# GpSimd subtracts the high parts of four weight chunks, and VectorE skips them

## What is computed

```
x = x + 0.5 * swiglu(rmsnorm(x, ff1_norm), ...)
h = rmsnorm(x, mix_norm);  proj = h @ w_in          # the mixer begins
...
y = gla_mixer(x, ...)                               # second block, layer 0
x = layer_norm(ALPHA * x + y, ...)
x = layer_norm(ALPHA * x + swiglu_ffn(x, ...), ...)
y = moba_mixer(x, positions, w_in, w_out)           # layer 1: block attention begins
...
```

## Time and profile before

| | |
|---|---|
| median of three runs | 1213.64 us (1212.88 to 1213.91) |
| the profiled execution's own time | 1213.54 us |
| its span, first to last instruction | 1211.5 us |
| TensorE busy | 1199.9 us (99%) |
| VectorE busy | 942.8 us (78%) |
| ScalarE busy | 678.2 us (56%) |
| GpSimd busy | 42.1 us (3%), 85 instructions |
| low parts of weights on VectorE (line 1765) | 476.6 us, 405 instructions, mean 1196 ns |

### The profile page before, as it was taken

How to read it: one execution, slowest core, us unless ns; L and a number is a source line. 1 busy time by engine, 2 the same in 40 slices (tenths; PEclk the granted TensorE clock), 3 DMA queues, 4 the chain that set the end, 5 groups by cost and what they waited for, 6 DMA issues and landing times.

```text
span 1211.5 us, 16276 instructions
## 1 busy us (share of the span) xinstructions
PE 1199.9 (99%) x6097; PEld 1008.9 (83%) x6097; DVE 942.8 (78%) x1396; ACT 678.2 (56%) x973; POOL 42.1 (3%) x85
## 2 busy tenths in 40 slices
PE   9999999999999999999999999999999999999997
PEld 7888888888788888888888888888887888888886
DVE  5999997756676666888987677786998777687797
ACT  6566655546666354665656554656554454566561
POOL 2000002100000000000010001000000000000000
PEclk9999999999999999999999999999999999999999
DMA  8666566754545556666557656566566544766652
GB/s 271 198 207 193 184 208 199 251 174 142 155 141 173 184 181 208 176 194 187 191 180 187 193 192 221 170 194 196 174 209 216 167 139 139 238 181 194 187 189 72
DMA packets 150654, 225.83 MB, mean 186 GB/s; under 512 B 8152, under 2 KB 85984, under 8 KB 150576
## 3 DMA queue, kind: packets, MB, share of 16 engines
q1 hardware_dynamic: 148048, 216.10, 56.8%
q0 software_dynamic: 2512, 8.69, 2.6%
q10 hardware_dynamic: 16, 0.00, 0.0%
HBM read 223.72 MB, written 1.05 MB: 186 GB/s over the span
## 4 chain that ended last, share of the span: by engine, by line
PE 95%; DVE 3%; DMA 0%; issue 0%; ACT 0%; SPq 0%; DVEq 0%
PE ps L689 23%; PE ps L601 16%; PE ps L616 16%; PE ps L608 16%; PE ps L693 12%; PE ps L526 3%; PE ps L671 2%; PE ps L666 2%; PE ps L669 2%; DVE wl L1765 1%; PE ps L856 1%; PE ps L869 1%; DMA raw<-in_ff_w_gate_dram 0%; DVE X L2025 0%; PE ps L1072 0%
## 5 line engine op out<-in xcount | busy, mean ns | idle before, releaser
L1765 DVE TENSOR_TENSOR wl<-raw,wh 128x1024 fp32r<-128x1024 f32 (+1 forms) x405 | 476.6, 1196 | 80.2 <-ACT wh L1143 78.1
L1143 ACT ACTIVATE wh<-raw 128x1024 fp32r<-128x1024 f32 (+1 forms) x405 | 408.5, 1032 | 58.5 <-PE ps L616 17.6
L689 PE MATMUL ps<-XT,wh 128*128 128x512 f32 x1216 | 422.9, 394 | 0.0
L693 PE MATMUL ps<-XT,wl 128*128 128x256 f32 x1216 | 338.0, 278 | 0.0
L689 PEld LDWEIGHTS ps<-XT,wh 128*128 128x128 f32 x1216 | 227.9, 187 | 52.3
L693 PEld LDWEIGHTS ps<-XT,wl 128*128 128x128 f32 x1216 | 228.8, 188 | 0.2
L601 PE MATMUL ps<-wh,XT 128*128 128x512 f32 x510 | 203.3, 399 | 0.0
L608 PE MATMUL ps<-wl,XT 128*128 128x512 f32 x510 | 199.4, 391 | 0.7 <-DVE wl L2604 0.7
L616 PE MATMUL ps<-wh,XT 128*128 128x512 f32 x510 | 158.0, 391 | 0.0
L601 PEld LDWEIGHTS ps<-wh,XT 128*128 128x128 f32 x510 | 95.8, 188 | 21.1 <-ACT wh L1694 0.6
L608 PEld LDWEIGHTS ps<-wl,XT 128*128 128x128 f32 x510 | 95.8, 188 | 20.7 <-DVE wl L2604 1.9
(11 more groups left out here) (339 smaller groups left out, 1412.3 us busy)
## 6 DMA issues: line engine op xcount, KB each, us to landing
raw<-in_ffn_w_gu_dram SPq DMA_DIRECT2D x88, 512.0 KB, 4.3
raw<-in_w_in_dram SPq DMA_DIRECT2D x56, 512.0 KB, 3.8
raw<-in_ff_w_up_dram SPq DMA_DIRECT2D x44, 512.0 KB, 4.4
raw<-in_ff_w_down_dram SPq DMA_DIRECT2D x44, 512.0 KB, 3.8
raw<-in_ffn_w_down_dram SPq DMA_DIRECT2D x44, 512.0 KB, 4.3
raw<-in_ff_w_gate_dram SPq DMA_DIRECT2D x40, 512.0 KB, 3.8
raw<-in_gla_w_in_dram SPq DMA_DIRECT2D x24, 512.0 KB, 4.6
raw<-in_moba_w_in_dram SPq DMA_DIRECT2D x24, 512.0 KB, 4.7
```

Of the source, the lines that this page charges most:

```text
L689: e.matmul(o, wh_of(j)[:, w], XT[:, kt, :, :].rearrange("p a n -> p (a n)"), start=kt == 0, stop=False)
L693: ins = e.matmul(o[:, 0:256], wl_of(j)[:, w], XTH[:, kt, :], start=False, stop=kt == kts - 1)
L1143: e.activation(wh_of(j)[:, 0:m], source(j), ACT.Copy).then_inc(S("wh"), 1)
L1765: e.tensor_tensor(wl_of(j)[:, 0:m], source(j), wh_of(j)[:, 0:m].bitcast(F32), ALU.subtract).then_inc(S("wl"), 1)
```

## The change

GpSimd gets a function `lows_of` that computes the low parts of the first two chunks of a product, each behind the wait for its high part, counting in a semaphore of its own, `wl_pool`. It is called for `vg0` early in GpSimd's program (ahead of the mixer's RMS norm) and for `mq0` ahead of the layer norm before the block attention. VectorE's `low_to` passes over these four chunks. All waits for a low part go through `low_ready`, which names the right semaphore and count.

```
+        pool_lows = [first_chunk(name) + i for name in ("vg0", "mq0") for i in range(2)]
+
+        def low_ready(j):
+            if j in pool_lows:
+                return S("wl_pool"), pool_lows.index(j) + 1
+            return S("wl"), j + 1 - sum(i < j for i in pool_lows)
...
             if r >= NR:                                  # load_chunk
-                e.wait_ge(S("wl"), loads[r - NR] + 1)
+                e.wait_ge(*low_ready(loads[r - NR]))
...
                 elif t == 0 and c == 0:                  # pe_products; other products alike
-                    e.wait_ge(S("wl"), j + 1)
+                    e.wait_ge(*low_ready(j))
...
                 while at_chunk["next"] <= min(last, len(chunks) - 1):   # low_to, VectorE
                     j = at_chunk["next"]
+                    if j in pool_lows:
+                        at_chunk["next"] += 1
+                        continue
...
+            def lows_of(name):                           # GpSimd
+                at = first_chunk(name)
+                for j in range(at, at + 2):
+                    e.wait_ge(S("wh"), j + 1)
+                    e.tensor_tensor(wl_of(j), source(j), wh_of(j).bitcast(F32), ALU.subtract).then_inc(S("wl_pool"), 1)
...
             load_g(mix_norm[0].partition_broadcast(P))
+            lows_of("vg0")
...
                 load_b(ln_b[i, k].partition_broadcast(P))
+                if stage == 6:
+                    lows_of("mq0")
                 layer_norm(stage)
```

More of the change, by code:

```diff
@@ L667, in pe_seven @@
                     if i == 0:
-                        e.wait_ge(S("wl"), j + c + 1)
+                        e.wait_ge(*low_ready(j + c))
                     e.matmul(o, lh, low[:, cols(i)], start=False, stop=False)
@@ L938, in pe_gla @@
             e.wait_ge(S(f"ev{bank_of('low', 0)}"), ev_count["low", 0] - 1)
-            e.wait_ge(S("wl"), at + 1)
+            e.wait_ge(*low_ready(at))
             for kt in range(8):
@@ L1742, in weight_sums @@
                 if g:
-                    e.wait_ge(S("wl"), max(i for i in group_of if group_of[i] == (g - 1, 3)) + 1)
+                    e.wait_ge(*low_ready(max(i for i in group_of if group_of[i] == (g - 1, 3))))
                 e.wait_ge(*source_ready(j))
```

## The result

The changed kernel takes 1217.37 us, the median of six runs (1217.07 to 1217.67), against 1213.44 for six runs of the kernel before. The ratio is 1.0032 with a 95% interval of 1.0022 to 1.0042: slower by 3.9 us. I had forecast 1218.0, slower, with a chance of 0.62. The profiled execution took 1217.26 us, its span is 1215.2.

The account below looks back on a forecast made before the run. TensorE bounds the kernel, with 2.0 us of gaps to win. GpSimd's subtracts delay VectorE by 4B, less 4.54 us saved: 4.4 us at B = 2.24, so 1213.54 becomes 1218.0 us, range 1211.2 to 1220.0.

Parts of the forecast that it names:

- The bound: TensorE, busy 1199.9 of 1211.5 us; closing its gaps at mixer (0.55) and block attention (1.45) gives at most 2.0 us.
- The length of a subtract: One GpSimd subtract of 128x1024 at either place takes 2.24 us, with 0.96 and 2.67 as ends.
- two passes and three: GpSimd handling a subtract's operands one after the other takes 1.81 us, or 2.67 if the write is a third pass.
- The collision: In VectorE's earlier trains, two-operand subtracts and GpSimd's reads exclude each other; VectorE waits for a whole GpSimd subtract.
- The sum: Both places together lose 4.4 us, 2.2 at the mixer and 2.2 at the block attention, giving 1218.0 us.
- 4B - 4.54: Net loss over both places: each train ends 2B later, less 2.27 us saved by two skipped subtracts; 4.4 us.
- B: Length of one GpSimd subtract, also taken as VectorE's wait for it at both places; 2.24 us.
- the wait for the turned x: Sign: waits of line 526 still there; at the mixer the low part of x freeing the transposes comes 2.21 us later.
- The later reloads: Loads behind 72, 73, 333 and 334 are issued 2 to 4.5 us later but cost nothing; chunk 338 has 3.7 us cover.
- No collision: Rival: VectorE and GpSimd read side by side, both gaps go, 2.0 us gained, 1211.5 us; chance 24 in 100.
- VectorE's train goes first: Rival: GpSimd gets in only when VectorE stops for something else; about 1214.1 us; 14 in 100 together with A quick subtract.
- A quick subtract: Rival: exclusion holds but B is short, nothing lost below 1.135 us; say 1214; 14 in 100 with VectorE's train goes first.

Follow-up runs that it names:

- the memset's trace: Changed kernel with GpSimd's four subtracts replaced by memsets of zeros, which write but read nothing; ratio 0.9988 to the kernel before.
- a copy's: Changed kernel with GpSimd's four subtracts replaced by copies from raw, one operand read; ratio 0.9991 to the kernel before.
- the last run of other tiles: VectorE does all subtracts as before; GpSimd adds four on norm weights, their tile placed where no other moves; ratio 1.0050, 1220.4 us.
- the block attention alone: Changed kernel with GpSimd subtracting only the block attention's two chunks, the mixer as in the kernel before; ratio 1.0020.
- the combined kernel: Against the kernel before: at the mixer VectorE's 75 and 76 moved behind an update, at the block attention GpSimd subtracts 335 behind the train; ratio 0.9986.
- The first run of other tiles: VectorE does all subtracts as before; GpSimd adds four on norm weights, with a new tile that moved most others; ratio 1.0129.

## Why the prediction was right

**The bound.** TensorE's waits were the only time to win. The gaps were worth 2.2 us, not 2.0: I took off eight transposes at their busy time of 1.03 us, but in the memset's trace, without the gap, they take 0.89 us of the distance between starts.

**The length of a subtract.** I took 2.24 us, the middle of two passes and three, and used it both as the subtract's length and as what VectorE waits. One takes 2.40 us where VectorE does not hold it up, and it holds VectorE for about 2.2. That the guess stood so near 2.2 is luck: no run shows passes, and a length of 2.40 put into the sum would have given 5.1 us. The hold is 0.2 us shorter than the instruction in all three forms: 2.2 of 2.40 us, 0.83 of a copy's 1.04, 1.06 of the 1.26 that an extra subtract takes at 903.48 in the last run of other tiles. The Trainium skill (GPSIMD Engine Reference, Performance versus the Vector engine) gives GpSimd 1.96 times VectorE's time for a two-input addition of 2048 elements; 2.40 against 1.22, 1.97 times, agrees.

**The collision.** This was the step with the least support: an affine select that had cost a scan 0.04 us. It held, in the order that the power beside VectorE's pair had shown: GpSimd gets in between two instructions that stand back to back.

**The sum.** 4B - 4.54 with B = 2.24 gave 4.4 us. With the trains as measured it is (7.88 - 3.49) + (7.66 - 3.49) - 4.54 = 4.0, and TensorE's steps at the two places sum to 4.03. Of the 0.4 us between, 0.2 is GpSimd's head start at the block attention (1.99 us of waiting in place of 2.2), and the rest is in B.

**Where it was wrong in detail.** I let TensorE stall once, 2.6 us at chunk 73, and named waits of two to three microseconds as the sign. It stalled for 72 as well (0.47 us of idling, then 1.66), as a low part 2.2 us late had to. And the wait for the turned x did not stay at the mixer: TensorE's stalls came to 2.7 us in place of 2.6 and VectorE's chain was 2.13 us late in place of 2.21, so that TensorE came just behind it. Neither changes the sum of delays, but the split was lucky: the sum has no term for TensorE's clock, and in the last run of other tiles a wait of 2.1 us and one of 2.6 us were each followed by 1.6 us lost to a lower clock. Whether one stall of 2.6 us at chunk 73 would have done the same, no run shows. The later reloads and GpSimd's own late work cost nothing, as forecast: no wait of TensorE names them.

**The rivals.** *No collision* fell with the trains of 7.9 us. *VectorE's train goes first* fell at 177.42, where GpSimd got in. *A quick subtract* was right about its condition: with the copy, at 0.83 us under the 1.135 of break-even, the same change pays 1.6 us by TensorE's steps, though the whole runs can't tell it.

## What to carry to other kernels

Before work moves from VectorE to an idle GpSimd, look at what VectorE runs at that moment and where its operands are: beside subtracts with two operands in SBUF a GpSimd instruction that read SBUF cost VectorE its own length less 0.2 us, so the move pays only if that is less than what VectorE saves (here 2.2 against 1.135 us, a loss); beside updates out of PSUM and statistics on one tile it was free. The idle time of GpSimd says nothing about this. The sign in the trace is a train of subtracts that grows longer without idle time (3.49 to 7.88 us), since the wait is inside the duration.

## What the runs showed of the hardware that I had not expected

In the last run of other tiles TensorE's granted clock fell from 1.00 to 0.50 (from 2.4 to 1.2 GHz) behind waits of 2.1 and 2.6 us, at 193.2 and 920.2, for 3.4 us each. In the changed kernel, behind the waits of 1.66 and 1.65 us, it stayed at 1.00 (the columns as above):

```profile
170.00:190.00 20.00, 17.87 (x82) 14.22 (x81) 18.48 (x19) 9.60 (x14) 6.29 (x2) 1.00 0.66 218
880.00:912.00 32.00, 29.87 (x131) 24.08 (x130) 30.40 (x31) 16.15 (x17) 5.71 (x2) 1.00 0.57 184
```

So there the collision cost more than the delay of VectorE's chain: the lower clock is 3.2 of the 7.4 us that TensorE's steps add at the two places.

In three traces TensorE's matmuls start 2% further apart for nearly a hundred microseconds, with a granted clock of 1.00, which costs 1.9 us each time: in the copy's from about 35 to 130, in that of the block attention alone from 760 to 860, and in the combined kernel's from 1050 to 1145, each away from the places that were changed. The first run of other tiles loses its 10 us at this rate or at about half of it, over most of its length. As none of the three moves a tile, moved tiles are not needed for it; its cause stays open.
